# Norms after four projections taken by halves of the tokens, and a bias table sent through GpSimd's queue

## The reference

```
def rms_norm(x, g):
    return x * rsqrt(mean(x * x, axis=-1) + eps) * g

for l in range(2):
    h = rms_norm(x, norm_g[l, 0])
    h = time_mix(h, ..., w_o_rwkv)          if l == 0
    h = swa_sink_attention(h, ..., w_o_attn) if l == 1
    x = x + rms_norm(h, norm_g[l, 1])       # post-norm, residual
    h = conv_ffn(rms_norm(x, norm_g[l, 2]), w_up[l], conv_w[l], conv_b[l], w_down[l])
    x = x + rms_norm(h, norm_g[l, 3])       # post-norm, residual
    if l == 0: k_sh, v_sh = shared_kv(x, kv_g, w_kv)
x = second_block(x, ...)                    # starts with rms_norm(x, e_norm) @ e_w_in
```

## Time and profile before

| what | value |
|---|---|
| median of 3 runs | 2403.3 us (2400.73 to 2409.46) |
| the profiled execution | 2408.64 us, of which the span is 2406.8 us |
| mean granted TensorE clock | 0.973 of full speed |
| PE busy | 2285.5 us (95%) |
| DVE, ACT, POOL busy | 1137.4, 641.5, 0.2 us |
| the chain that ended last, by engine | PE 90%, DVE 5%, ACT's queue 2%, ACT 1%, DMA 1% |
| moved by DMA | 154.70 MB, mean 64 GB/s |

### The profile page before, as it was taken

How to read it: one execution, slowest core, us unless ns; L and a number is a source line. 1 busy time by engine, 2 the same in 40 slices (tenths; PEclk the granted TensorE clock), 3 DMA queues, 4 the chain that set the end, 5 groups by cost and what they waited for, 6 DMA issues and landing times.

```text
span 2406.8 us, 37808 instructions
## 1 busy us (share of the span) xinstructions
PE 2285.5 (95%) x15102; PEld 1463.6 (61%) x15102; DVE 1137.4 (47%) x2599; ACT 641.5 (27%) x1407; POOL 0.2 (0%) x4
## 2 busy tenths in 40 slices
PE   7999999998899999999988699999899998999998
PEld 3555555554488888855443588888545654444553
DVE  7455555541666662154234466632444464222542
ACT  2222222211323320045321133310220353113540
POOL 0000000000000000000000000000000000000000
PEclk9999999999999999999889899999999998999998
DMA  3100000002222222111113222231211110221111
GB/s 107 57 32 32 32 32 32 20 19 106 70 77 84 86 98 97 66 45 44 53 53 94 80 84 87 94 120 66 105 70 70 44 45 36 70 70 53 36 36 70
DMA packets 25275, 154.70 MB, mean 64 GB/s; under 512 B 2476, under 2 KB 2604, under 8 KB 11308
## 3 DMA queue, kind: packets, MB, share of 16 engines
q1 hardware_dynamic: 22032, 145.57, 16.9%
q10 hardware_dynamic: 3100, 7.08, 1.0%
HBM read 146.61 MB, written 6.03 MB: 63 GB/s over the span
## 4 chain that ended last, share of the span: by engine, by line
PE 90%; DVE 5%; ACTq 2%; issue 1%; ACT 1%; DMA 1%; DVEq 0%; SPq 0%
PE banks L1637 17%; PE banks L1238 11%; PE banks L1106 8%; PE banks L1151 7%; PE banks L2135 5%; PE banks L1987 3%; PE banks L491 3%; PE banks L459 3%; PE banks L481 2%; ACTq L2440 2%; PE banks L2021 2%; PE banks L1594 2%; PE banks L1999 2%; PE banks L2718 2%; PE banks L596 2%; PE banks L1609 1%
## 5 line engine op out<-in xcount | busy, mean ns | idle before, releaser
L1637 PE MATMUL banks<-arena 128*128 128x256 f32 x2016 | 439.7, 380 | 26.1 <-ACT arena L1692 25.1
L1637 PEld LDWEIGHTS banks<-arena 128*128 128x128 f32 x2016 | 383.3, 190 | 83.0 <-ACT arena L1692 25.7
L1238 PE MATMUL banks<-arena 128*128 128x256 f32 x1232 | 266.6, 378 | 0.0
L1238 PEld LDWEIGHTS banks<-arena 128*128 128x128 f32 x1232 | 232.6, 189 | 33.7
L1106 PE MATMUL banks<-arena 128*128 128x512 f32 x448 | 196.2, 599 | 0.0
L1151 PE MATMUL banks<-arena 128*128 128x512 f32 x384 | 168.3, 595 | 0.0
L1692 ACT ACTIVATE arena<-banks 128x256 f32<-128x256 f32 x180 | 69.1, 385 | 309.9 <-PE banks L1637 295.2
L1106 PEld LDWEIGHTS banks<-arena 128*128 128x128 f32 x448 | 85.6, 192 | 108.4 <-issue 108.2
L1860 DVE SCALAR_TENSOR_TENSOR arena<-arena 128x511 f32<-128x511 f32 (+1 forms) x144 | 108.2, 751 | 72.9 <-ACT arena L1701 55.8
L2056 ACT ACTIVATE arena<-arena 128x128 f32<-128x128 f32 (+3 forms) x192 | 101.5, 530 | 122.3 <-DVE arena L2088 122.1
L2088 DVE CUSTOM_DVE_ANT_0 arena<-banks,arena 128x256 f32<-128x256 f32 (+3 forms) x160 | 70.9, 472 | 132.5 <-PE banks L1987 131.9
(11 more groups left out here) (310 smaller groups left out, 3024.2 us busy)
## 6 DMA issues: line engine op xcount, KB each, us to landing
arena<-up SPq DMA_DIRECT2D x44, 1024.0 KB, 4.8
arena<-down SPq DMA_DIRECT2D x16, 1408.0 KB, 6.2
arena<-w_mix SPq DMA_DIRECT2D x8, 1728.0 KB, 7.2
arena<-e_in SPq DMA_DIRECT2D x12, 1024.0 KB, 4.8
arena<-o_in SPq DMA_DIRECT2D x8, 1024.0 KB, 4.8
arena<-w_o SPq DMA_DIRECT2D x4, 1024.0 KB, 4.7
arena<-q SPq DMA_DIRECT2D x8, 512.0 KB, 3.4
arena<-o_attn SPq DMA_DIRECT2D x4, 1024.0 KB, 4.8
```

What stands on the lines that cost most here:

```text
L1238: ins = pe.matmul(ps[:, bank, LO], w[:, t, :], x[:, t, :], start=first and t == 0, stop=t == FT // 2 - 1, skip_group_check=not first)
L1637: ins = pe.matmul(out, w[:, q, :], x[:, q, :], start=start and q == 0, stop=q == 3, skip_group_check=not start)
```

## The change

First, bridges 0 to 3 take their post-norm by halves of the tokens.

- The second half of w_o and of o_attn (tiles 4 to 7) is done by `tensor_halves`: four tiles on LO, then the same four on HI, 256 columns a matmul. The LO half's sum (named 10) stands behind the first four steps of HI's first tile, its spread six steps later.
- The last turn of the down projections runs P1, P4, P6, P2, P7, P5, P3. With P7 the LO half is complete; the sum stands inside P5, the spread behind it, and P3 (in bank 2 now) follows.
- DVE and ACT norm the LO half (steps t0, x0, g0) while PE does the HI half, then HI (t1, x1, g1) while PE does the LO half of the next projection's slabs 0 and 1 (`halves_after`; in kv, the keys and the values of blocks 0 and 1). The HI sum (11) stands inside slab 0's LO part, its spread behind it.
- The squares of the second norm go to k.h, which is free then, instead of two alternating buffers.
- Pairs 2 and 3 of up lie in banks 2, 3 and 6, 7 instead of 4 to 7. DVE makes all of h and the first two rescalings before its first taps.
- x is loaded again before the last slab of w_o instead of after it.

Second, the four `bias_out` transfers and `bias_in` are issued by GpSimd: the four when layer 1's gated tiles number 4, 8, 12 and 16 (of 22), the last one after bridge 3's `keep`. ACT issues none.

```diff
-        for s in range(2):
-            self.slab(pe, name, 1, s, k.h)
+    def tensor_halves(self, pe, name, source, bridge, n, loaded=None):
+        k, base = self.k, BASE[name]
+        for h, half in enumerate((LO, HI)):
+            for j in range(4):
+                s, m = j // 2, j % 2
+                if h == 0:
+                    pe.wait_ge(k.landed[s], 16 * (TURN[name] + 2))
+                    pe.wait_ge(self.copied, 4 + base + j + 1)
+                else:
+                    pe.wait_ge(bridge.half_copied, 4 * n + j + 1)
+                for t in range(KT):
+                    ins = pe.matmul(k.ps[:, j, half], k.ring[s][:, (m * KT + t) * P:(m * KT + t + 1) * P], source[:, t, half],
+                                    start=t == 0, stop=t == KT - 1)
+                    if h == 0 and j == 0 and t == 0:
+                        k.begun(ins, 0)
+                    if h == 1 and j == 2 and t == 0:
+                        k.begun(ins, 1)
+                    if t == KT - 1:
+                        ins.then_inc(bridge.half_summed, 1)
+                    if h == 1 and j == 0 and t == 3:
+                        if loaded:
+                            loaded()
+                        bridge.sum_tensor(pe, n, "10")
+                    if h == 1 and j == 1 and t == 1:
+                        bridge.spread_tensor(pe, n, "10")
     def landed_tensor(self, pe, name, n):
...
+    def halves_after(self, pe, name, bridge, n, first_bank, summed, slot_begun):
...
+                             bridge.xg[n][:, t, half], start=t == 0, stop=t == KT - 1)
+        pe.wait_ge(k.landed[0], (TURN[name] + 1) * 16)
+        for t in range(KT):
+            bridge.wait_half(pe, n, 0, t)
+            for m in range(2):
+                ins = half_slab(0, 0, m, t)
+                if slot_begun and m == 0 and t == 0:
...
+                    k.begun(ins, 0)
+            if t == 3:
+                bridge.sum_tensor(pe, n, "11")
+        bridge.spread_tensor(pe, n, "11")
+        pe.wait_ge(k.landed[1], (TURN[name] + 1) * 16)
+        for m in range(2):
+            for t in range(KT):
+                half_slab(1, 0, m, t)
+        for t in range(KT):
+            bridge.wait_half(pe, n, 1, t)
+            for m in range(2):
+                ins = half_slab(0, 1, m, t)
+                if t == KT - 1:
+                    ins.then_inc(summed, 1)
+        bridge.sum_tensor(pe, n, "2")
+        for m in range(2):
+            for t in range(KT):
+                ins = half_slab(1, 1, m, t)
+                if m == 0 and t == 0:
+                    k.begun(ins, 1)
+                if m == 0 and t == 5:
+                    bridge.spread_tensor(pe, n, "2")
+            ins.then_inc(summed, 1)
     def first_vector(self, dve, name, j, dst, bridge):
...
+                product("P2", 2, two, actv[:, 1::2, LO], True, odd_ready)
             pe.wait_ge(k.landed[1], (TURN[name] + q + 1) * 16)
             if turn:
...
+                pe.wait_ge(A.sem, A.at(turn, "u2"))
+                pe.wait_ge(W.sem, W.at(turn, "S4"))
+                product("P7", 0, self.s["S3"], self.t["T3"], False, None, both_free)
                 pe.wait_ge(J.sem, J.at(turn - 1, "c12"))
-            product("P5", 1, self.s["S1"], self.t["T1"], True, at_first)
-            pe.wait_ge(A.sem, A.at(turn, "u2"))
-            product("P7", 0, self.s["S3"], self.t["T3"], False, at_first)
-            pe.wait_ge(A.sem, A.at(turn, "p5"))
-            product("P3", 1, self.s["S4"], actv[:, 1::2, HI], False, at_first)
-    def scalar(self, act, layer, o, ss, sq, added):
-        ps, S, A, J = self.k.ps, self.products, self.parts, self.joined
-        for q in range(4):
...
+FULL = [4, 6, 4, 6]
+def square_after(n, m):
+    return {-1: 0, 2: 1, 6: 2, 7: 3}.get(m) if n % 2 == 0 else {-1: 0, 4: 1}.get(m)
+def add_after(n, m):
+    return {-1: 0, 2: 1, 6: 2, 7: 3}.get(m) if n % 2 == 0 else {1: 0, 5: 1}.get(m)
...
-        self.dve.done(dve.tensor_tensor(self.ss, self.ss, self.sq[m % 2], ALU.add), f"{n}.{name}{m}")
+        if name == "b" and n < 4:
+            q = self.k.h
+            ins = dve.tensor_tensor(self.ss, q[:, 0, :] if m == 1 else self.ss, q[:, m, :], ALU.add)
+        else:
...
+    def normed_half_vector(self, dve, n, h, m):
...
+                self.normed_half_vector(dve, n, 0, m)
+                if m and n in (1, 3) and m - 1 == 4:
+                    self.down.late_vector(dve, n // 2, self, n, "P3")
+                i = add_after(n, m - 1) if m else None
+                if i is not None:
+                    self.add_half_vector(dve, n, 1, i)
+            self.inverse_vector(dve, n, "11")
+            dve.wait_ge(self.pe.sem, self.pe.at(0, f"{n}.spread11"))
+            for m in range(KT + 1):
+                self.normed_half_vector(dve, n, 1, m)
                 if m >= 3:
                     self.add_vector(dve, n, "b", m - 2)
         else:
...
+    def bank(pair, m):
+        return (4, 6, 2, 6)[pair] + m
...
+        def keys(h, half):
...
+        bridge.spread_tensor(pe, 1, "11")
+        pe.wait_ge(k.landed[1], 16 * (TURN["kv"] + 1))
+        for b in range(2):
+            values(b)
+        keys(1, HI).then_inc(self.kv_pe, 1)
+        bridge.sum_tensor(pe, 1, "2")
+        for b in range(2, QB):
+            ins = values(b)
         ins.then_inc(self.kv_pe, 1)
...
         k, lin, name = self.k, self.lin, "e_in"
-        lin.tensor_after(pe, name, self.bridge, 3, 1)
+        for m in range(4):
+            pe.wait_ge(lin.copied, BASE[name] + m + 1)
+        lin.halves_after(pe, name, self.bridge, 3, 0, lin.summed, False)
         ring, slot = lin.landed_tensor(pe, name, 2)
...
             stream(sp, k, "w_mix")
-            stream(sp, k, "w_o")
+            stream(sp, k, "w_o", 0, 3)
             sp.wait_ge(mix.tail_dve.sem, mix.tail_dve.at(PAIRS - 1, "gated"))
             sp.dma_start(k.x, ins["x"]).then_inc(xin, 16)
+            stream(sp, k, "w_o", 3, 4)
...
-            bridge.joined_tensor(pe, 0)
+            lin.tensor_halves(pe, "w_o", k.h, bridge, 0, lambda: pe.wait_ge(small, 48))
...
             win.tensor(pe, bridge)
             sec.setup_tensor(pe)
-            lin.tensor(pe, "o_attn", k.at(MIX0, KT, T), 2, lambda t: pe.wait_ge(win.out.sem, win.out.at(t, "x")))
-            bridge.joined_tensor(pe, 2)
...
             bridge.scalar(act, 2)
-            up.scalar(act, 1, conv, bridge, 2, lambda part: sec.bias_out(act, part))
...
+        @block.gpsimd
+        def _(pool):
+            for part in range(4):
+                pool.wait_ge(up.used, 2 + FT + PLAIN * (part + 1))
+                sec.bias_out(pool, part)
+            pool.wait_ge(bridge.act.sem, bridge.act.at(0, "3.keep"))
+            sec.bias_in(pool)
```

More of the change, by code:

```diff
@@ L1432, in root_scalar @@
-    def root_scalar(self, act, n, which):
-        r, _ = self.factors(which)
-        act.wait_ge(self.pe.sem, self.pe.at(0, f"{n}.sum{which}"))
-        self.act.done(act.activation(r, self.k.ps[:, self.banks[n][0], 0:QB], ACT.Sqrt, bias=self.k.eps, scale=1.0 / D),
-                      f"{n}.root{which}")
+        for b in blocks:
+            ins = pe.matmul(self.k.ps[:, bank, b:b + 1], self.ss[:, b * P:b * P + P], ones[:, 0:1], start=b == blocks[0],
+                            stop=b == blocks[-1])
@@ L1597, in slab @@
                     k.begun(ins, s)
-                if between and m == 0 and t == 3:
-                    between()
             ins.then_inc(self.summed, 1)
```

507 lines of the change are left out of this document (309 added, 198 removed).

## The result

The changed kernel takes 2381.78 us (median of 4 runs, 2365.67 to 2383.13); the kernel before, on the same chip, 2406.38 us. The ratio is 0.9885, interval 0.9836 to 0.9933: 25 us won by the medians, 28 by the ratio. The forecast was 2340 us in a range of 2322 to 2374 us, so the result lies outside the range. The profiled execution took 2380.81 us, against 2408.64 us before.

The account below looks back on a forecast made before the run. PE, busy 95% of the span, bounds the kernel, so only its idle or slow time can be won. 2408.6 - 40.5 (bridges) - 38.5 (ACT's queue) + 16 (collisions) = 2345.6 us, 2340 us against the median; range 2322 to 2374 us.

Parts of the forecast that it names:

- The bridges' own gaps: Bridges 0 to 3: PE's gaps and the slow clock behind them go, a net gain of 40.5 us.
- So I take no new wait: Bridges 0 to 3: other work keeps up with the new order; half of the gain lost if all covers fail.
- PE's clock stays up in gaps this short: Bridges: argument against the late-halves rival; a missed cover costs only its own size, tenths to 2 us.
- rival of late halves: Bridges: the halves don't keep up, half of the gain lost, 20 us, giving 2361 us; chance 0.08.
- Layer 1's 38.5 us: Layer 1, second spread to down: excess over layer 0, blamed on transfers holding ACT's queue, counted as won.
- on POOL nothing stands behind them, so the queue no longer matters: Layer 1's bias transfers: issued by GpSimd, they hold up no evictions, so the 38.5 us are won.
- the stop was never ACT's queue but the transfers: Rival, layer 1: the edit misses the cause of PE's stop, 38.5 us stay, 2363 us; chance 0.03.
- The collisions: Layer 1's sevens: slab loads beside bias transfers land late, 13 loads at 1.2 us each, 16 us lost.
- Its threshold: Layer 1's slab loads: a landing up to 10.1 us is covered, each us beyond is one lost.
- rival of 45 to 55 us: Layer 1: transfers collide harder, 3.5 to 5 us a load, time about 2373 us; chance 0.14.
- The rival by which GpSimd is kept from writing its descriptors: Layer 1: slower than before; one mechanism is GpSimd locked out of SBUF during DVE copies; 2493 us, chance 0.05.
- Landings of 8 to 12.5 us for some 13 of 18: Sign in the profile after: layer 1 slab loads land so; wrong if they stay at 4.8 or exceed 15 us.

Follow-up runs that it names:

- before_repl16: Kernel before, transfers still on ACT; the 12 lines go to DRAM once and are copied from there, 32 x 12 rows each: 2370.3 us, ratio 0.9844.
- best: Changed kernel with h awaited tile by tile behind bridges 1 and 3 and the bias lines copied from DRAM, 32 x 12 rows: 2327.57 us, ratio 0.9673.
- fixed: Changed kernel with h awaited tile by tile behind bridges 1 and 3, e_in's 72-column tiles reordered: 2364.83 us, ratio 0.9832.
- before_no_outs: Kernel before without the four transfers of the bias lines; the read-back takes the same bytes from a weight: 2371.44 us, ratio 0.9858.
- one_line: Changed kernel with each of the four transfers cut from three lines to one, 128 rows; read-back from a weight: 2341.01 us, ratio 0.9725.
- spread12: Changed kernel with each transfer taking all 12 lines 32 times from SBUF in place of three lines 128 times: 2343.21 us, ratio 0.9739.
- pool_only: Kernel before with only the five bias transfers moved to GpSimd: 2409.71 us, ratio 1.0002.
- dram3: Changed kernel with the transfers' shape kept, three lines 128 times, but the source in DRAM in place of SBUF: 2341.2 us, ratio 0.9733.
- rerun: Changed kernel once more, without an edit: 2381.01 us.

## Why the prediction was wrong, point by point

**The bridges' own gaps: right.** The sum had 40.5 us for them; the runs before_repl16 and best, which have neither the dear transfers nor the new wait, lie 42.7 us apart by the medians, 42.1 us by the profiled executions and 41 us by the ratios. The covers that were thin held: no wait at the first norm's sums, none at the scaled tiles, no late slab at bridges 0 and 2, and the clock is up behind them. Bridges 1 and 3 have their first norm hidden too.

**"So I take no new wait": the first step that failed.** I went through every cover of the first norm and of the HI half and stopped at the second sum. The second norm's path was not checked, since the change does not touch it: keep, two rescalings and eight tiles of h, 0.61 + 1.30 + 5.30 us on the chain above. Its cover was touched. Before, 10.3 us of work stood behind the second spread (24 records of 512 columns at bridge 3, 48 of 256 at bridge 1); after, 20 of 256, 4.32 us, because the pieces of slab 1 that could stand there were spent between first sum and second. In up the next product (L1838) reads h as soon, but tile by tile, each tile for 0.86 us of PE's work (two records of 0.43), and DVE makes three tiles of h before its rescalings (629.47 to 631.55 us, behind the spread that ended at 628.73): no wait. In kv the next product asks for all eight tiles at once, behind two rescalings. In e_in it asks tile by tile, but two records of 72 columns take 0.25 us where DVE makes a tile in 0.66. In bridge 1 the wait is 3.04 us, and the 20 records behind it take 11.84 us where the chain of the kernel fixed has 8.58: 6.3 us. In bridge 3, 17.81 us pass from the spread's end (1698.30) to the first wide tile (1716.11), where the records between need about 12.1 us (12.2 in the kernel fixed), and eight wide records take 6.09 in place of 3.63 us: 8.2 us. Together 14.5 us. The kernel fixed got 17 us back by the medians and 13 us by the ratios, so the 14.5 us agree with it within the noise. "PE's clock stays up in gaps this short" failed at bridge 3, where the gaps were of 0.16 to 0.22 us. My rival of late halves (20 us) had nearly the size, but at the wrong place.

**Layer 1's 38.5 us: read right, put down wrong.** The transfers are its cause, as before_no_outs shows. But "on POOL nothing stands behind them, so the queue no longer matters" took the engine that PE waited for as the cause. ACT's issue was slow because the transfer was, as before_repl16 shows: with transfers that land in 7.3 us (median of four) the same queue issues one in 0.54 us. The rival "the stop was never ACT's queue but the transfers" is what happened, and its price, 38.5 us kept, was right within 1 us. Its chance of 0.03 rested on the chain of waits alone, which names the last releaser and not why that one was late.

**The collisions: the term that was mis-sized, 16 us against 37.5.** Its threshold held in the changed kernel: the eight landings above less 10.1 us each give 11.7 + 1.6 + 3.0 + 1.8 + 2.9 + 1.8 + 12.9 + 2.7 = 38.4 us, and the stretch lost 37.5. It is rough elsewhere: in one_line a load of 9.9 us is on the chain and 1.1 us are lost, and spread12 lost 7.3 us where its four loads less 10.1 us each make 4.9. Both factors of 13 loads x 1.2 us were off: 8 loads were hit, at 4.7 us each. The 1.2 us came from the loads of 12.5 and 7.8 us in the earlier trace rows, and I left the row of 19.5 us out of the mean because its transfer "was stuck in issue"; two of the eight new ones were of that kind, and they make 24.7 of the 38.4 us. The other six, 11.7 to 13.1 us, were like the row of 12.5 us, which I had halved with a row that cost nothing. The sum's upper bound (71 us) and the rival of 45 to 55 us enclosed it from above, the range took in 50 us of collisions, but not 37.5 us of them together with 14.5 us of new wait. The rival by which GpSimd is kept from writing its descriptors is not what happened: from the same queue 384 rows landed in 5.7 us once they came from DRAM.

**The sum again**, with the sizes measured: 2408.6 - 40.5 - 38.5 + 37.5 + 14.5 = 2381.6 us, against 2380.81 us profiled. That the second and third terms cancel is what pool_only shows, 1.0002. Against the median the forecast had 5.3 us less, since the profiled execution before lay that much above it; with the measured sizes that gives 2376.3 us, and the 5.5 us from there to 2381.78 come almost wholly from this step, since the profiled execution after did not lie above its median but 1 us below.

**The signs named ahead.** "Landings of 8 to 12.5 us for some 13 of 18" was wrong in both numbers; "over 5 us of waits" at the bridges did not show as waits (3.04 us and some tenths) but did as time, since the clock fell behind them. The transfers started 64.5, 52.7 and 52.6 us apart and not 48, since they wait for the sevens that they themselves delay.

## What to carry to other kernels

When work is pulled ahead of a wait, list what stood behind each later wait as its cover and count it again, those of untouched waits too. When an engine is late because it issues a transfer, look first at why the transfer is slow (its landing, its source, over how many rows it is dealt) and only then at which queue issues it; moving it only moves the name in the list of waits. A price taken from a few collisions should include the dearest one unless a row, not a reason, excludes it: two loads of eight made 24.7 of 38.4 us here.

## What the runs showed of the hardware

Four transfers that repeat 3 SBUF rows 128 times (960 KB) took 30.9 to 44.1 us (median 37.2), 22 to 32 GB/s, and slowed the slabs' loads beside them from 4.8 to between 11.7 and 23.0 us. The same shape from DRAM took 18.8 us and left them at 9.0 us at most. The busy share of the 16 DMA engines, in windows of the changed kernel and of one_line and spread12 (us, busy time and count of PE, PEld, DVE, ACT and POOL; granted clock, DMA share, GB/s):

```profile
1308.00:1318.00 10.00, 0.57 (x1) 0.50 (x2) 0.58 (x1) 0.00 (x0) 0.00 (x0) 0.67 0.16 37
```

```profile
1343.00:1352.00 9.00, 9.00 (x43) 7.89 (x42) 6.04 (x11) 3.48 (x7) 0.00 (x0) 1.00 0.85 30
```

```profile
1339.00:1354.00 15.00, 15.00 (x71) 13.14 (x70) 8.99 (x16) 4.07 (x9) 0.67 (x1) 1.00 0.70 97
```

From three rows 0.16 of the engines are busy, which is near 3 of 16; from twelve, 0.70; from one row dealt by its 128 copies, 0.85, at only 30 GB/s. (The window of spread12 has slab loads in it too.) The Trainium skill, "DMA: Bandwidth & Descriptors", section "Why a DMA increments its semaphore by 16 and not by 1", says that the number of engines is the largest up to 16 that divides the slowest dimension of both sides: 3, 12 and 16 here, and the shares agree. Yet one SBUF row read with 0.85 of the engines busy gave no more than three rows did (24 GB/s against 22 to 32, over the whole landing). The runs point to two things that meet in the dear transfer, few engines and slow reads of few SBUF rows. Few engines alone (dram3) left the loads at 9.0 us or less and slow reads alone (one_line, with a third of the bytes) at 9.9, both below 10.1 us. Two rivals are left: a transfer that lands in 14 to 19 us is simply beside the loads for a shorter time, and a transfer from DRAM keeps off SBUF, where the slabs are written; no run takes either apart. Why such reads are slow was not tried. The two transfers beside the latest loads were also the slowest, 43.1 and 44.1 us against 31.3 and 30.9, and why the loads beside the first and the fourth transfer (21.8 and 23.0 us, and in rerun 21.88 and 23.13) are so much later than beside the second and third (13.1, 13.0) stays open.
